# Stage seams of a two-block transformer kernel: projections ahead of the first recurrence unit, more of them behind the last, a third place for the queries' weights, and two ScalarE operations in other places

## The reference, cut to what matters

```
u = rmsnorm(h, g_pre);  proj = u @ w_in            # in tiles of 128 columns
feat_a, z_a, c_q, c_kv, k_pe, z_b, gate_logits = split(proj)
y_a = rwkv7_branch(feat_a, z_a, ...)               # a recurrence over the tokens, 8 heads of 64
q  = rmsnorm(c_q) @ w_uq;  kv = rmsnorm(c_kv) @ w_ukv     # latent attention: queries, keys, values
y_b = (causal attention of q, kv) * silu(z_b) @ w_out_b
gates = sigmoid(gate_logits + b_gate)
merged = g_a * y_a + g_b * y_b
h = h + rmsnorm(merged @ w_o, g_post)
```

## Time and profile before

| | us |
|---|---|
| median of three runs | 1934.61 |
| the profiled execution, its own time | 1933.76 |
| its span in the trace | 1931.9 |
| PE busy | 1845.6 (96%) |
| DVE, ACT, POOL busy | 956.7, 793.1, 415.3 |
| granted TensorE clock, mean | 0.993 |

### The profile page before, as it was taken

The page is one execution under the profiler, slowest core; times in us unless marked ns, Lnnn a source line. Parts: engine busy times, 40 slices in busy tenths (PEclk is TensorE's granted clock), DMA queues, the critical chain, the costliest instruction groups (busy, mean ns, idle before and its releaser), DMA issues.

```text
span 1931.9 us, 38784 instructions
## 1 busy us (share of the span) xinstructions
PE 1845.6 (96%) x16241; PEld 1523.1 (79%) x16241; DVE 956.7 (50%) x2088; ACT 793.1 (41%) x1757; POOL 415.3 (21%) x416
## 2 busy tenths in 40 slices
PE   6999999999997999989999999999998989999998
PEld 6997766888885999877777777877776876667898
DVE  5677766143346144035555455555555146775514
ACT  5346666243345133233333333334332256555421
POOL 4550000111114232312222222222222101001221
PEclk9999999999999999999999999999999999999999
DMA  5153310423332422331221211212112230005432
GB/s 186 46 179 81 87 28 1 129 85 113 114 111 64 153 77 91 112 94 44 70 80 59 64 59 59 67 61 61 59 51 86 68 101 12 1 1 185 159 125 88
DMA packets 148853, 159.91 MB, mean 83 GB/s; under 512 B 14948, under 2 KB 132008, under 8 KB 148680
## 3 DMA queue, kind: packets, MB, share of 16 engines
q1 hardware_dynamic: 148456, 156.44, 25.5%
q0 software_dynamic: 224, 0.99, 0.2%
HBM read 110.53 MB, written 52.62 MB: 84 GB/s over the span
## 4 chain that ended last, share of the span: by engine, by line
PE 78%; DVE 7%; ACT 6%; DMA 4%; POOL 3%; issue 2%; SPq 0%; POOLq 0%; DVEq 0%; ACTq 0%
PE ps L684 9%; PE ps L685 9%; PE ps L686 9%; PE ps L956 7%; PE ps L958 6%; PE ps L957 6%; PE ps L1064 4%; PE ps L794 3%; PE ps L773 3%; PE ps L781 3%; PE ps L1101 2%; PE ps L1250 2%; DMA t<-in_w_in 2%; PE ps L1273 2%; PE ps L1260 1%
## 5 line engine op out<-in xcount | busy, mean ns | idle before, releaser
L684 PE MATMUL ps<-t,t 128*128 128x256 f32 (+2 forms) x1392 | 433.7, 312 | 11.4 <-DVE t L2142 4.2
L2717 POOL TENSOR_TENSOR t<-t,t 128x512 fp32r<-128x512 f32 x183 | 238.7, 1320 | 919.9 <-ACT t L1349 854.7
L685 PE MATMUL ps<-t,t 128*128 128x256 f32 (+2 forms) x1392 | 426.9, 307 | 0.0
L686 PE MATMUL ps<-t,t 128*128 128x256 f32 (+2 forms) x1392 | 426.8, 307 | 0.0
L956 PE MATMUL ps<-t,t 128*128 128x512 f32 (+2 forms) x720 | 292.0, 405 | 0.7 <-ACT t L1625 0.7
L684 PEld LDWEIGHTS ps<-t,t 128*128 128x128 f32 x1392 | 268.1, 193 | 29.6 <-issue 16.2
L686 PEld LDWEIGHTS ps<-t,t 128*128 128x128 f32 x1392 | 267.8, 192 | 10.8
L685 PEld LDWEIGHTS ps<-t,t 128*128 128x128 f32 x1392 | 268.2, 193 | 10.3 <-issue 0.2
L958 PE MATMUL ps<-t,t 128*128 128x512 f32 (+2 forms) x720 | 269.0, 374 | 0.0
L957 PE MATMUL ps<-t,t 128*128 128x512 f32 (+2 forms) x720 | 268.5, 373 | 0.0
L1349 ACT ACTIVATE t<-t 128x512 fp32r<-128x512 f32 x182 | 107.5, 624 | 151.0 <-DMA t<-in_w_in 88.8
(11 more groups left out here) (266 smaller groups left out, 2906.5 us busy)
## 6 DMA issues: line engine op xcount, KB each, us to landing
t<-in_w_in SPq DMA_DIRECT2D x53, 512.0 KB, 5.8
zgate_spill<-t SPq DMA_DIRECT2D x20, 512.0 KB, 3.2
tile_bias<-t SPq DMA_DIRECT2D x16, 576.0 KB
t<-tile_bias SPq DMA_DIRECT2D x8, 1152.0 KB, 6.1
t<-in_x SPq DMA_DIRECT2D x16, 512.0 KB, 9.4
t<-zgate_spill SPq DMA_DIRECT2D x16, 512.0 KB, 3.9
feat_spill<-t SPq DMA_DIRECT2D x13, 512.0 KB, 3.2
tile_bias<-band_bias SPq DMA_DIRECT2D x48, 128.0 KB
```

The source lines that it names most:

```text
L684: e.matmul(dst, lh, rh, start=k == 0, stop=False)
L685: e.matmul(dst, lh, rl, start=False, stop=False)
L686: m = e.matmul(dst, ll, rh, start=False, stop=k == n - 1)
L2717: e.tensor_tensor(WLO[wslot(b)][:, o], WST[:, o], WHI[wslot(b)][:, o].bitcast(F), ALU.subtract).then_inc(w_lo.sem, w_lo.up((b, p)))
```

## The change

Five edits. Every program gets the same order, so each edit stands in several of them.

1. A unit 0 yields LOAD_US ahead of its stage 0, on all engines, behind the loads that SP issues and POOL's first columns; LOAD_US becomes 9, OFFSET 15, and the extra 8 us behind the first stage is gone. The extra 0.8 us falls behind the stages 1 to 8 of the list.
2. The steps of `late` that are left when both flows are done have a fill of 2.2 us in place of 0.7.
3. `w_uq` (UKV+1) gets the third place; its parts wait for the end of the recurrence on every engine. The blocks behind it change places. During block UKV-1 `tick` may also split parts of UKV+1.
4. ACT's square of the centered output moves one stage forward, to the stage of "center".
5. In the merge, ACT takes the gate of u+1 behind the first half of u, ahead of the copy of the second half, in place of taking it at the head of u+1.

```
-            return 2 if b == OUT1 + 3 else (b + (b > OUT1 + 3)) % 2
+            return 2 if b in (OUT1 + 3, UKV + 1) else (b + (b > OUT1 + 3) + (b > UKV + 1)) % 2
+        def wplace(b):
+            return "attention b" if b == OUT1 + 3 else "recurrence"
 ...
-                while self.coming is not None and self.coming[0] <= self.b + (2 if self.b == OUT1 + 1 else 1) and self.ticks[0] >= 20 + 9 * self.ticks[1]:
+                while self.coming is not None and self.coming[0] <= self.b + (2 if self.b in (OUT1 + 1, UKV - 1) else 1) and self.ticks[0] >= 20 + 9 * self.ticks[1]:
 ...
-        ... LOAD_US, OFFSET = ..., 8, 14
+        ... LOAD_US, OFFSET = ..., 9, 15
 ...
-                    self.fill(next(flows[0]) + (LOAD_US if n == 0 else 0.8 if n < 8 else 0))
+                    self.fill(next(flows[0]) + (0.8 if 0 < n < 9 else 0))
 ...
                 for _ in self.late:
-                    self.fill(0.7)
+                    self.fill(2.2)
 ...                                  # in unit(), all five programs, ahead of stage 0
+                if u == 0:
+                    yield LOAD_US
 ...                                  # weight parts, ACT and POOL
                 if wslot(b) == 2:
                     for q in EVERY:
-                        w.wait_ge(*q["attention b"])
+                        w.wait_ge(*q[wplace(b)])
 ...                                  # ACT, end of a unit
-                yield NORM_US
                 w.wait_ge(*norm2_v[u, "yc"])
                 w.wait_ge(*inv_v[u, "z2"])
                 e.activation(E1[:, :], S.YT[:, :], ACT.Square)...
+                yield NORM_US
                 yield STAGE_US
 ...                                  # ACT, merge
+            def output_gate(u):
+                br, n = MERGES[u // 2]
+                w.wait_ge(*d_ga[u % 2][u])
+                e.activation(GA[u % 2][:, :], GA[u % 2][:, :], ACT.Sigmoid, bias=vec("b_gate", 8 * br + 2 * n + u % 2))...
 ...
-                    w.wait_ge(*d_ga[u % 2][u])
-                    e.activation(GA[u % 2][:, :], ..., ACT.Sigmoid, ...)...
+                    if u == 0:
+                        output_gate(0)
 ...
                     for half in range(2):
                         wt.tick(12)
+                        if half and u + 1 < 2 * len(MERGES):
+                            output_gate(u + 1)
                         if br == 0:
                             w.wait_ge(*merge_v[x, c, half, "sum"])
                             e.activation(AH[:, ct, half512(half)], M2[half][:, :], ACT.Copy)...
```

More of the change, by code:

```diff
@@ L548, in a_scored @@
             return 8 * (i // 2) + 5 + 2 * (i % 2)
-        STAGE_US, NAT_US, GRAM_US, INV_US, PLAN_US, CHAIN_US, NORM_US, LOAD_US, OFFSET = 0.94, 1.1, 0.8, 0.6, 0.7, 0.67, 0.54, 8, 14
+        STAGE_US, NAT_US, GRAM_US, INV_US, PLAN_US, CHAIN_US, NORM_US, LOAD_US, OFFSET = 0.94, 1.1, 0.8, 0.6, 0.7, 0.67, 0.54, 9, 15
         LANDED = 6
@@ L1860, in act_program @@
             w.wait_ge(*vec_v["vec"])
+            def output_gate(u):
+                br, n = MERGES[u // 2]
+                w.wait_ge(*d_ga[u % 2][u])
+                e.activation(GA[u % 2][:, :], GA[u % 2][:, :], ACT.Sigmoid, bias=vec("b_gate", 8 * br + 2 * n + u % 2)).then_inc(
+                    merge_a.sem, merge_a.up(("gate", u)))
             for x, (br, n) in enumerate(MERGES):
@@ L1866, in act_program @@
                     ct = 2 * n + c
-                    w.wait_ge(*d_ga[u % 2][u])
-                    e.activation(GA[u % 2][:, :], GA[u % 2][:, :], ACT.Sigmoid, bias=vec("b_gate", 8 * br + ct)).then_inc(merge_a.sem, merge_a.up(("gate", u)))
+                    if u == 0:
+                        output_gate(0)
                     if x < 2:
```

## The result

The changed kernel took **1948.18 us** in the median of four runs (1945.90 to 1950.47), the kernel before 1934.44 in four runs beside it. The ratio is 1.0072, with a 95% interval of 1.0055 to 1.0090: slower by 13.7 us, where the forecast had 1924.6 and its range ended at 1930.5. The profiled execution of the changed kernel took 1950.2 us (before 1933.76).

What follows compares the result with a forecast made beforehand. PE was taken to bound the kernel (busy 1845.6 of 1931.9 us), so only its waits could shrink. Terms -5.0 + 0.5 + 0 + 0.3 + 0.8 - 5.1 - 1.5 = -10.0 us gave 1924.6 as median, range 1919.5 to 1930.5.

Steps and rivals of the forecast that it cites:

- The shift that follows: Units stand 1 to 3 steps later against the weight parts; eight collisions at the spread, 0.54 us each: +0.5 us.
- Rival 4: Slower: POOL's weight part stands ahead of every spread, 23 more waits of up to 0.98 us: +22.5, 1947; chance 0.04.
- Right: Signs: first spread wait about 1 us, clock 1.0; square's and merge's waits gone; queries' 4.9; first L1180 3 to 4.
- Wrong: Signs: POOL's four parts in one piece before the first power, first turn without wait, or spread waits above 7 us outside seams.
- Edit 1, first unit: PE's wait at the first spread falls from 4.58 to 1.0 us, and 1.4 of slow matmuls go: -5.0 us.
- Edit 2, seam: Behind the last unit: moved steps cost 0; PE begins the first turn 2.3 us later with 2.05 us more behind: +0.3.
- Edit 3: Queries' weights: the third part stands behind POOL's "latent ready", so PE goes on 0.8 us later: +0.8 us.
- Edit 4: ACT's square ahead of copies that wait for PE removes seven waits of 0.59 us and one of 0.99: -5.1 us.
- Edit 5: End of the merge: gates are there before their products, so PE's wait for the low part goes: -1.5 us.
- Rivals 1 to 3: First wait only moves, 1929.6, chance 0.15; late chain covered, 1919, 0.10; queries' wait and slow clock go, 1918, 0.05.
- the forecast's flat 1.4 us: Estimated second payment in slow matmuls behind a long PE wait, at the first unit and behind the last: 1.4 us each.

Runs made afterwards that it cites:

- experiment 1: Kernel before with 9.8 instead of 8 us for the projections ahead of the first unit (the shifted kernel): 1957.27 us against 1933.85.
- experiment 8: Kernel before with 9.8 instead of 8 us and the gate's load 11 stages earlier in 12 of 16 units: 1946.94 us.
- experiment 3: Changed kernel with the gate's load 11 stages earlier in 12 of 16 units: 1934.57 us against 1933.85 for the kernel before.
- experiments 9 to 11: Weight parts taken later: in the kernel of experiment 3, 1938.55 us; of experiment 8, 1938.65; in the changed kernel with 11 us and earlier gate's load, 1938.22.
- experiment 5: Kernel before with 8.35 instead of 8 us ahead of the first unit, one dense step more: 1940.32 us, ratio 1.0039.

## Why the prediction was wrong

**The step that failed** is the paragraph "The shift that follows", **+0.5 us** with bounds of -3 and +4. By itself the shift costs +23.4 (experiment 1). The step asked how the units then stand against the weight *parts* and priced a collision by the mean of those of before (0.54). It left out two other things that come at fixed steps, the *store* and the *fetch* of a block. Both stand in SP's order, and there the gate's load has its place among them. My sentence that the first unit's loads are issued in the same order answered this for unit 0 alone; it wasn't asked for units 1 to 15. A count of steps to the block's end, as above, would have shown three units going over the edge. The price was wrong as well where the mechanism was the one that I had. In the changed kernel the waits for the spread outside the two seams are seven with 7.9 us (10.2 less 1.67 and less 0.61), where I had eight with 4.3; one of them, behind a part that stood for its fetch, is 2.66.

**Rival 4** named the shift as the mechanism that could make the kernel slower, gave it 0.04, and priced it at +22.5 by POOL's part ahead of every spread. That 22.5 lies near 23.4, and its 1947 near the measured 1948.2, is chance. The waits for the spread were 8.9 us in the shifted kernel, 9.4 before; 10.3 us of the time went by the gate's load (experiment 8; 13.6 in the changed kernel, experiment 3), and 8.3 more went when the parts came later (experiments 9 to 11). A mean of small collisions says nothing of a large one: a part held by a fetch costs PE 2.6 to 3.3 us, not 0.54. That the kernel before stood at an edge, the count shows for that kernel alone: three of its gate loads stand 0 steps from a store and a fetch.

All five signs under "Right" came true (a first wait of 1.67 us at a clock of 1.00, no waits for the square, 0.3 us left at the merge, 4.64 at the queries, 3.43 at L1186), and so did one under "Wrong": 7.9 us of waits for the spread outside the seams, over the 7 named. The right signs looked only at the places that the edits aim at, so they could not see a loss elsewhere.

**The other terms**, by the runs:
- Edit 1, first unit, -5.0: the wait fell from 4.58 to 1.67 (1.0 forecast) and the clock from 0.83 to 1.00. The step's mechanism was right at its place. But most of it didn't reach the end. At the old phase some 1 us did (1928.66 against 1929.54, less than the intervals tell apart). PE's busy time of 800 to 900 us is 91.9 before, 93.9 in the changed kernel (new waits of 0.98 us at 856 and 1.43 at 884), and 97.1 with a pause of 11 us; there the whole time is 3.4 under edits 2 to 5 alone.
- Edit 2, seam +0.3: the first L1186 waits 3.43, as "3 to 4" said, and the first two scalings took 1.35 and 1.28 us beside POOL's parts, as the followed chain had them; a later one took 0.34. The wait of L1161 ahead of it came from unit 15's gate. It wasn't run alone.
- Edit 3, +0.8: the wait grew by 0.6 (4.64 against 4.06); in the time it is nothing measurable.
- Edit 4, -5.1: -6.3 and -6.1 measured. The nine small waits add up in full, at both places; that it is some 1 us more than the term is inside the interval.
- Edit 5, -1.5: the wait went from 1.48 to 0.3, -1.2. It wasn't run alone.
- Edits 2 to 5 together: -4.3 measured, -5.5 forecast, inside the interval (-5.6 to -2.1).

Rivals 1 to 3 didn't come about: the first wait shrank, the late chain wasn't covered, the queries' wait grew.

**What stays open**: why one dense step more (experiment 5) costs 6.9 us without a late gate. Its trace shows more short waits for the spread and a later seam, but none of them was taken away by itself. Nor was the order on SP's queue split from the store's wait: experiment 3 moved the load ahead of both. How the 13.1 us that the earlier gate's load leaves of the shift divide is also not settled, since moving the parts moved other waits.

## What to carry to other kernels

When two streams are interleaved by an order that is written out, every edit that gives one of them a few steps moves all that follows against the other. Count for every periodic item of the one stream (stores and fetches on the DMA queue as well as compute) whether it passes an item of the other, before and after the edit, and price each crossing by the longest thing it can be held by, a whole fetch. A small load that an engine needs soon belongs on the queue ahead of a large one that is needed later. And when a schedule constant is touched, time a few values of it: here 8, 8.35, 9.8 and 11.8 in the same kernel gave 1933.9, 1940.3, 1957.3 and 1933.4 us.

## What the runs showed of the hardware

- The gate's load of unit 3, behind a fetch of 1 MB on the same queue, took 6.4 us from issue to landing. All 16 of these loads, first in the kernel before, then in the changed one, by the view of their line:

```profile
DMA to landing us min/median/max: 2.3/4.4/6.7
```

```profile
DMA to landing us min/median/max: 2.7/5.3/6.8
```

  In the changed kernel the nine that were issued directly behind a fetch of 1 MB took 5.3 to 6.8 us, the other seven 2.7 to 4.4. In the kernel before there were six behind a fetch, with 5.4 to 6.7 us, and eight of the other ten took 2.3 to 3.5.
- The clock behind a wait is not a fixed price. Behind the 3.9 us at 1012 it took 31% and 38% of two stretches of 5 us, 3.4 us. Behind the 4.1 us at 1498 it took 34% of two such stretches (1495 to 1505), 3.4 us again. In the shifted kernel, behind the same wait of 3.9 us (at 1017), it was 25% and 9%, 1.7 us. The rows are first those behind the waits at 1208 and 1308 of the changed kernel, then the shifted kernel's:

```profile
1210.00:1215.00 5.00, 4.89 (x29) 0.67 0.02 3
...
1305.00:1310.00 5.00, 2.35 (x44) 0.89 0.00 0
1310.00:1315.00 5.00, 5.00 (x42) 0.77 0.08 26
```

```profile
1015.00:1020.00 5.00, 3.00 (x44) 0.75 0.22 72
1020.00:1025.00 5.00, 5.00 (x103) 0.91 0.04 12
```

  The waits of 2.8 and 2.7 us at 1208 and 1308 cost 1.7 us each (33% of a stretch; 11% and 23% of two). So the forecast's flat 1.4 us is a little small for these and too small for those at 1012 and 1498.
